# Hybrid decoder layer: inverse softmax sums turned through memory instead of by TensorE, grouped values and scores, new order tables

## Chip, cores and metric

One core of one Trainium2 chip. The metric is the device time of one execution in microseconds (us). The kernel before takes 304.36 us, the median of 3 runs (304.03 to 304.5).

## What is computed

One pre-norm decoder layer over 256 tokens of width 1024, 16 heads of 64. Eight heads (group 0) do causal attention, since one block of 256 keys is all there is; eight heads (group 1) do a mixture of three dilated windows, which here is one softmax with a mask that carries the logarithm of how many windows see a key.

```python
h = rmsnorm(x, attn_norm)
qkv = einsum('bsd,de->bse', h, w_in)            # 1024 x 3072
q, k = rope(q), rope(k)
o_moba = moba_attention(q[:8], k[:8], v[:8])    # group 0
o_dil = dilated_mixture(q[8:], k[8:], v[8:])    # group 1
mixed = concatenate([rmsnorm(o_moba, ...), rmsnorm(o_dil, ...)])
x = x + mixed @ w_out                           # 1024 x 1024
h = rmsnorm(x, ffn_norm)
x = x + (silu(h @ w_gate) * (h @ w_up)) @ w_down   # 1024 x 2816, 2816 x 1024
return rmsnorm(x, final_norm)
```

## The kernel before

**Weights.** All weights stream as blocks of 128 x 512 through a ring of 12 slots (`raw`), four blocks (a quad, 1 MB) per transfer, issued by SyncE (`quad`, L363). Each pair of blocks is split in two rounded parts: ScalarE writes `w_hi` (`split_hi`, L725), VectorE `w_lo`, the rest (`split_lo`, L939). For each block and each half of the tokens TensorE makes three matmuls of 512 columns (`three_pass`, L437 to L439): a block is six of them. Blocks 0 to 47 are the q/k/v projection, 48 to 63 the output projection (group 0 in 48 to 55, group 1 in 56 to 63; of every four blocks all first halves come before all second halves), from 64 on the feed-forward part. A quad is loaded once VectorE has split the last pair that its slots held.

**Attention between the blocks.** The tables `PE_PLAN`, `DVE_PLAN`, `ACT_PLAN` and `PLACE` say behind which block (or slot of the loop that splits pairs) an engine does an item of attention. In the slot of odd number i ScalarE splits pair (i+9)/2, VectorE pair (i+7)/2, after the items of that slot; TensorE needs pair p for block 2p. The items, for group g:

- `rope` (VectorE), `turn` (TensorE transposes q or k, L464; ScalarE and VectorE split the result), `score` u = 0, 1, 2 (TensorE L485 to L490; VectorE adds the mask and takes the maximum, L1032; ScalarE takes the exponential and its sums, L820).
- `squares` (VectorE, L1043): transposes the 32 x 32 squares of one of 12 tiles of probabilities; SyncE then gathers that tile with four transfers of 64 KB (`place_probs`, L403) into one of six landing places.
- `values` (TensorE, L511): values times probabilities, u = 0 for the first half of the tokens, u = 1, 2 for the second. Both halves use bank 7, so each must be taken out before the next is written.
- `rsum`: the inverse of the softmax sums. VectorE inverts (L1048), GpSimd widens them to 128 x 512 (L1234), TensorE transposes them by four transposes (L525), ScalarE copies them to `rsums_turned` (L829). Four times in all (two groups, two halves).
- `norm` (VectorE, L1054): values times `rsums_turned`. `o` (ScalarE L836, L842) and `olo` (VectorE, L1067) split the result; GpSimd adds its squares; `osum` (TensorE, L532) sums them over the features.
- `residual` (VectorE, L1078) adds an output-projection result to `x`; `ffnturn` transposes it for the feed-forward part (TensorE L447, ScalarE L744, VectorE L950).

Every engine works strictly through its own list: an item that waits holds all splits and items behind it.

Of the kernel before, what the change touches and what calls it, by code (L numbers as in the profile page):

```python
# [24 lines left out]
P = 128  # L25
# [40 lines left out]
RSUM_BANK = 7, 6  # L66
# [17 lines left out]
SQ = 32  # L84
# [33 lines left out]
    43: [("values", 0, 1), ("values", 0, 2)],
    45: [("score", 1, 2), ("rsum", 1, 0)],
    50: [("values", 1, 0)],  # L120
    51: [("osum", 0), ("rsum", 1, 1)],
    54: [("values", 1, 1), ("values", 1, 2)],
    58: [("osum", 1)],
    61: [("ffnturn", 0), ("ffnturn", 1)],
# [19 lines left out]
    34: [("turn", 1, 0, 1), ("rsum", 0, 1)],
    37: [("turn", 1, 1, 0)],
    39: [("turn", 1, 1, 1), ("score", 1, 0)],
    40: [("squares", 1, 0), ("squares", 1, 1)],
    41: [("rsum", 1, 0), ("norm", 0, 0), ("score", 1, 1)],
    42: [("squares", 1, 2)],
    43: [("squares", 1, 3), ("norm", 0, 1)],  # L150
    44: [("olo", 0, 0)],
    45: [("score", 1, 2), ("olo", 0, 1)],
    48: [("squares", 1, 4), ("rsum", 1, 1), ("squares", 1, 5)],
    49: [("norm", 1, 0)],
    50: [("osum", 0), ("residual", 0)],
    51: [("olo", 1, 0)],
    53: [("norm", 1, 1), ("olo", 1, 1)],
    54: [("residual", 1)],
    56: [("osum", 1), ("residual", 2)],
    60: [("ffnturn", 0), ("ffnturn", 1)],  # L160
    61: [("residual", 3)],
# [3 lines left out]
    11: [("scale", 0)],  # L165
    12: [("scale", 1)],
    15: [("turn", 0, 0, 0)],
    17: [("turn", 0, 0, 1)],
    21: [("turn", 0, 1, 0)],
    23: [("turn", 0, 1, 1)],  # L170
    24: [("score", 0, 0)],
    27: [("score", 0, 1)],
    28: [("score", 0, 2)],
    30: [("turn", 1, 0, 0)],
    36: [("turn", 1, 0, 1)],
    37: [("rsum", 0, 0)],
    38: [("turn", 1, 1, 0), ("rsum", 0, 1), ("turn", 1, 1, 1)],
    39: [("take", 0)],
    42: [("score", 1, 0)],
    43: [("o", 0, 0), ("score", 1, 1)],  # L180
    44: [("o", 0, 1)],
    46: [("take", 1), ("score", 1, 2)],
    48: [("rsum", 1, 0), ("rsum", 1, 1), ("o", 1, 0)],
    52: [("o", 1, 1)],
    61: [("ffnturn", 0), ("ffnturn", 1)],
    62: [("residual", 2)],
# [13 lines left out]
def build(nc, x, first, weights, gains, final_norm, table, out):  # L200
# [3 lines left out]
    with ctx:  # L204
# [35 lines left out]
        sums = sb("sums", [P, 2, SH, GH])  # L240
        rsums = sb("rsums", [P, 2, SH, GH])
# [116 lines left out]


        @block.sync  # L360
        def _(sp):
# [35 lines left out]
            def place_probs(T):  # L397

                sp.wait_ge(p_turned, T + 1)
                if T >= LANDINGS:  # L400
                    sp.wait_ge(valued, (T - LANDINGS) // 2 + 1)
                for i in range(JS):
                    sp.dma_start(landed[:, T % LANDINGS, i, :],  # L403
                                 p_squares[i * SQ:(i + 1) * SQ, T % SQUARES, :, :]).then_inc(in_p[T % LANDINGS], 16)

            for r in range(2, HR):
                for pos in range(NQ):
                    ring_quad(r, pos)
                    for T in PLACE.get((r, pos), ()):
                        place_probs(T)  # L410
# [23 lines left out]
        def _(pe):  # L434
# [16 lines left out]
            def item(it):  # L451
# [15 lines left out]
                elif kind == "score":  # L467
# [6 lines left out]
                    if done:  # L474
                        pe.wait_ge(max_ready, done)
# [16 lines left out]
                elif kind == "values":  # L492
# [23 lines left out]
                elif kind == "rsum":  # L516
# [3 lines left out]
                    if n:  # L520
                        pe.wait_ge(rsum_taken, n)
# [808 lines left out]
```

## Time and profile before

| | |
|---|---|
| median of 3 runs | 304.36 us |
| the profiled execution, its own time | 304.51 us |
| its span (first to last instruction) | 302.7 us |
| TensorE busy | 294.1 us, 97% |
| VectorE, ScalarE, GpSimd busy | 67%, 55%, 6% |
| granted TensorE clock, mean | 0.994 |
| bytes moved by DMA | 61.65 MB, 204 GB/s |

The span is cut out of the execution's own time; 1.8 us lie around it. Matmuls overlap each other, so that the starts of two matmuls tell more of the time of one than its duration does.

### The profile page before, as it was taken

How to read it: one execution, taken by the hardware profiler on the slowest of the kernel's cores; microseconds unless marked ns; L12 is line 12 of the kernel's file. 1: busy time of each engine (PE TensorE's matmuls, PEld its weight loads, DVE VectorE, ACT ScalarE, POOL GpSimd, SP SyncE). 2: the span in 40 equal slices, each digit the busy share in tenths (PEclk: the TensorE clock that was granted, in tenths of full speed). 3: DMA queues.
4: the chain of work that ended last, by engine and by line, in shares of the span. 5: the costliest groups of instructions: out<-in, count | busy, mean ns of one | idle time of the engine just before them, and what ended most of it. 6: DMA issues, size and time to landing. Idle time of an engine off the chain costs nothing.

```text
span 302.7 us, 4335 instructions
## 1 busy us (share of the span) xinstructions
PE 294.1 (97%) x1448; PEld 240.0 (79%) x1448; DVE 203.7 (67%) x332; ACT 166.9 (55%) x283; POOL 19.3 (6%) x29
## 2 busy tenths in 40 slices
PE   8999999999999899999999999999999999999992
PEld 4688877887788688888888888888888888888882
DVE  3889999977898589729755555637465655455454
ACT  4877775829686549816554445354363545444224
POOL 0011000030333120200000000000000000000010
PEclk9999999999999999999999999999999999999997
DMA  7998445851695535765876566575656564651003
GB/s 255 422 423 302 178 178 141 266 140 79 172 372 177 187 135 150 277 236 210 269 266 207 226 186 264 173 241 174 207 176 249 174 267 159 238 200 28 0 0 139
DMA packets 21757, 61.65 MB, mean 204 GB/s; under 512 B 2545, under 2 KB 13809, under 8 KB 15601
## 3 DMA queue, kind: packets, MB, share of 16 engines
q1 hardware_dynamic: 21312, 60.70, 57.5%
q10 hardware_dynamic: 432, 0.80, 0.7%
q8 instruction: 7, 0.11, 0.1%
q14 instruction: 6, 0.04, 0.0%
HBM read 54.67 MB, written 1.05 MB: 184 GB/s over the span
## 4 chain that ended last, share of the span: by engine, by line
PE 82%; ACT 5%; DMA 5%; issue 3%; DVE 2%; SPq 2%; POOL 0%; POOLq 0%; ACTq 0%; DVEq 0%
PE bank L437 27%; PE bank L439 26%; PE bank L438 26%; DMA raw<-in_weights 2%; DMA room<-in_first 2%; ACT w_hi L725 1%; SPq L403 1%; DMA room<-room 1%; ACT probs L820 1%; PE bank L464 1%; ACT vals L793 1%; PE bank L447 1%; DVE xs L1152 0%; ACT o_hi L836 0%; DVE w_lo L939 0%
## 5 line engine op out<-in xcount | busy, mean ns | idle before, releaser
L725 ACT ACTIVATE w_hi<-raw 128x1024 fp32r<-128x1024 f32 x94 | 98.0, 1056 | 81.2 <-PE bank L439 72.2
L939 DVE TENSOR_TENSOR w_lo<-raw,w_hi 128x1024 fp32r<-128x1024 f32 x94 | 112.3, 1217 | 17.1 <-ACT w_hi L725 15.7
L437 PE MATMUL bank<-w_hi,x_hi 128*128 128x512 f32 x270 | 106.8, 396 | 0.6 <-DVE w_lo L967 0.6
L439 PE MATMUL bank<-w_hi,x_lo 128*128 128x512 f32 x270 | 105.2, 390 | 0.0
L438 PE MATMUL bank<-w_lo,x_hi 128*128 128x512 f32 x270 | 105.2, 390 | 0.0
L437 PEld LDWEIGHTS bank<-w_hi,x_hi 128*128 128x128 f32 x270 | 50.7, 188 | 12.3 <-DVE w_lo L967 1.4
L439 PEld LDWEIGHTS bank<-w_hi,x_lo 128*128 128x128 f32 x270 | 50.7, 188 | 10.6
L438 PEld LDWEIGHTS bank<-w_lo,x_hi 128*128 128x128 f32 x270 | 50.7, 188 | 10.1
L437 PE MATMUL bank<-w_hi,h_hi 128*128 128x512 f32 (+1 forms) x82 | 31.6, 385 | 0.0
L439 PE MATMUL bank<-w_hi,h_lo 128*128 128x512 f32 (+1 forms) x82 | 31.5, 384 | 0.0
L438 PE MATMUL bank<-w_lo,h_hi 128*128 128x512 f32 (+1 forms) x82 | 31.5, 384 | 0.0
L1095 DVE SCALAR_TENSOR_TENSOR rope_a<-bank,rstd,rope_b 128x256 f32<-128x256 f32 x22 | 9.8, 480 | 30.3 <-ACT rope_b L862 30.3
L1113 DVE TENSOR_TENSOR h_lo<-room,h_hi 128x512 fp32r<-128x512 f32 x10 | 6.9, 692 | 23.2 <-ACT h_hi L867 23.2
L437 PEld LDWEIGHTS bank<-w_hi,h_hi 128*128 128x128 f32 x82 | 15.4, 188 | 3.1
L438 PEld LDWEIGHTS bank<-w_lo,h_hi 128*128 128x128 f32 x82 | 15.4, 188 | 3.1
L439 PEld LDWEIGHTS bank<-w_hi,h_lo 128*128 128x128 f32 x82 | 15.4, 188 | 3.0
L820 ACT ACTIVATE probs<-probs,neg_max 128x128 f32<-128x128 f32 (+1 forms) x32 | 14.1, 447 | 4.6 <-DVE neg_max L1032 4.6
L437 PE MATMUL bank<-w_hi,o_hi 128*128 128x512 f32 (+1 forms) x42 | 16.5, 392 | 0.0
L439 PE MATMUL bank<-w_hi,o_lo 128*128 128x512 f32 (+1 forms) x42 | 16.0, 380 | 0.0
L438 PE MATMUL bank<-w_lo,o_hi 128*128 128x512 f32 (+1 forms) x42 | 15.9, 379 | 0.0
L862 ACT ACTIVATE rope_b<-bank,rstd 128x256 f32<-128x256 f32 x22 | 9.6, 464 | 4.1 <-PE bank L439 4.1
L1210 POOL TENSOR_SCALAR msq<-ssq 128x2 f32<-128x2 f32 (+1 forms) x2 | 0.4, 192 | 175.3 <-ACT junk L754 175.3
(101 smaller groups left out, 245.6 us busy)
## 6 DMA issues: line engine op xcount, KB each, us to landing
raw<-in_weights SPq DMA_DIRECT2D x47, 1024.0 KB, 4.8
room<-room SPq DMA_DIRECT2D x88, 64.0 KB, 2.1
room<-in_first SPq DMA_DIRECT2D x3, 384.0 KB, 5.1
room<-in_first SPq DMA_DIRECT2D x1, 1024.0 KB, 7.5
xs<-in_x SPq DMA_DIRECT2D x2, 512.0 KB, 9.3
out<-rot SPq DMA_DIRECT2D x3, 256.0 KB, 2.0
room<-in_first SPq DMA_DIRECT2D x1, 640.0 KB, 8.6
vals<-in_final_norm ACTq DMA_DIRECT2D x1, 512.0 KB, 7.2
```

The source lines that it names most:

```text
L403: sp.dma_start(landed[:, T % LANDINGS, i, :], p_squares[i * SQ:(i + 1) * SQ, T % SQUARES, :, :]).then_inc(in_p[T % LANDINGS], 16)
L437: pe.matmul(dst, a_hi, w1, start=first, stop=False)
L438: pe.matmul(dst, a_hi, w2, start=False, stop=False)
L439: return pe.matmul(dst, a_lo, w1, start=False, stop=last)
L447: ins = pe.transpose(dst[:, a * SEQ + s * P:a * SEQ + (s + 1) * P], xs[:, s, kt * P:(kt + 1) * P], ident)
L464: ins = pe.transpose(bank[TURN_BANK[qk_i][s]][:, p * P:(p + 1) * P], rot[:, qk_i, s, p * P:(p + 1) * P], ident_ja if qk_i else ident)
L725: act.activation(w_hi[:, slot:slot + 2, :], raw[:, slot:slot + 2, :], ACT.Copy).then_inc(hi_ready, 1)
L820: ins = act.activation(piece, piece, ACT.Exp, bias=neg_max[:, g, half, head:head + 1], scale=-1.0, accum_out=sums[:, g, half, head:head + 1])
L862: act.activation(silu[:, s, :], bank[4 + s][:, 0:FC], ACT.Silu, scale=rstd[:, 6 + s:7 + s]).then_inc(silu_done, 1)
L939: dve.tensor_tensor(w_lo[:, slot:slot + 2, :], raw[:, slot:slot + 2, :], w_hi[:, slot:slot + 2, :].bitcast(f32), ALU.subtract).then_inc(lo ...
L1095: dve.scalar_tensor_tensor(hid[:, s, :], bank[4 + s][:, FC:2 * FC], rstd[:, 6 + s:7 + s], silu[:, s, :], ALU.mult, ALU.mult).then_inc(hid_ ...
L1113: dve.tensor_tensor(hidden[1], placed, hidden[0].bitcast(f32), ALU.subtract).then_inc(ht_lo, 1)
```

## The change

1. **Inverse sums.** GpSimd's widening, TensorE's four times four transposes and ScalarE's four copies are gone. VectorE inverts, then transposes the 32 x 32 squares of all 32 sums (a 128 x 32 piece, `rsum_squares`). SyncE writes it to a tensor in HBM (`sums_out`, one transfer, pieces of 128 bytes) and reads it back, each row broadcast to 64 partitions (`sums_back`, two transfers of 128 KB, pieces of 512 bytes). `norm` waits for that.
2. **Banks.** The values of the first half go to bank 7, those of the second to bank 6; the late scores (u = 2) go to banks 6 and 7 instead of 4 and 5. So all three `values` of a group stand behind one block, and two `score` stand together.
3. **ScalarE issues** the gathers of the tiles 9 and 11; SyncE keeps the other ten.
4. **All four tables** are laid out anew.

```diff
-RSUM_BANK = 7, 6
+VALUE_BANK = 7, 6
+SCORE_BANKS = (4, 5), (4, 5), (6, 7)
...
 PE_PLAN = {
-    41: [("values", 0, 0), ("score", 1, 1)],
-    43: [("values", 0, 1), ("values", 0, 2)],
+    41: [("values", 0, 0), ("values", 0, 1), ("values", 0, 2)],
+    42: [("score", 1, 1), ("score", 1, 2)],
...
+    53: [("osum", 0), ("values", 1, 0), ("values", 1, 1), ("values", 1, 2)],
...
-    61: [("ffnturn", 0), ("ffnturn", 1)],
+    62: [("ffnturn", 0), ("ffnturn", 1)],
...
 DVE_PLAN = {
+    43: [("olo", 0, 0), ("olo", 0, 1)],
...
+    50: [("norm", 1, 0), ("residual", 0), ("norm", 1, 1)],
...
 ACT_PLAN = {
+    44: [("place", 9)],
+    45: [("take", 1)],
+    47: [("place", 11)],
...
+PLACE = {
...
+    (4, 2): [("back", 2), ("out", 3)],
+    (5, 0): [("place", 10)],
+    (5, 1): [("back", 3)],
 }
...
+        turned_sums = nc.dram_tensor("turned_sums", (2 * SH, SQ, P), f32, kind="Internal")
...
+            def sums_out(n):
+
+                sp.wait_ge(rsum_ready, n + 1)
+                sp.dma_start(turned_sums[n, :, :].rearrange("c (i a) -> i c a", a=SQ),
+                             rsum_squares[:, n, :]).then_inc(out_sums[n], 16)
+
+            def sums_back(n):
+
+                sp.wait_ge(out_sums[n], 16)
+                if n < SH:
+                    sp.wait_ge(turned, 6)
+                else:
+                    sp.wait_ge(o_ready, n - 1)
+                for r in range(2):
+                    sp.dma_start(rsums_turned[64 * r:64 * r + 64, n % 2, :].rearrange("d (p q) -> d p q", q=P),
+                                 turned_sums[n, n * GH + r:(n + 1) * GH:2, :].partition_broadcast(64)).then_inc(in_sums[n], 16)
...
                     if u == 0:
                         pe.wait_ge(v_taken, 2 * g + 2)
-                        pe.wait_ge(rsum_taken, 2)
-                    if u in (0, 1) and g + u:
-                        pe.wait_ge(o_ready, g * 2 + half)
+                    if g and u == 0:
+                        pe.wait_ge(max_ready, 2 * SC_TILES)
+                    elif u == 1 and not g:
+                        pe.wait_ge(qk_lo, 8)
...
-                                dst = bank[7][64 * r:64 * r + 64, head // 2 * P:(head // 2 + 1) * P]
+                                dst = bank[VALUE_BANK[half]][64 * r:64 * r + 64, head // 2 * P:(head // 2 + 1) * P]
...
-                elif kind == "rsum":
-                    _, g, s = it
-                    n = g * 2 + s
-                    pe.wait_ge(rsum_wide, n + 1)
...
-                    for p in range(HPAIRS):
-                        ins = pe.transpose(bank[RSUM_BANK[g]][:, p * P:(p + 1) * P], rsums_wide[s][:, p * P:(p + 1) * P], ident)
-                    ins.then_inc(rsum_turned, 1)
...
-                    act.activation(rsums_turned[:, s, :], bank[RSUM_BANK[g]][:], ACT.Copy).then_inc(rsum_taken, 1)
...
+                elif kind == "place":
+                    T = it[1]
+                    act.wait_ge(p_turned, T + 1)
+                    act.wait_ge(valued, (T - LANDINGS) // 2 + 1)
+                    for i in range(JS):
+                        act.dma_start(*place(T, i)).then_inc(in_p[T % LANDINGS], 16)
...
-                    dve.reciprocal(rsums[:, g, half, :], sums[:, g, half, :]).then_inc(rsum_ready, 1)
+                    n = g * 2 + half
+                    dve.wait_ge(inverted, n + 1)
+                    dve.reciprocal(rsums[:, g, half, :], sums[:, g, half, :]).then_inc(inverted, 1)
+                    dve.wait_ge(inverted, n + 2)
+                    dve.transpose(rsum_squares[:, n, :], rsums[:].rearrange("p g s h -> p (g s h)")).then_inc(rsum_ready, 1)
...
-                    dve.wait_ge(rsum_taken, n + 1)
+                    dve.wait_ge(in_sums[n], 32)
                     dve.wait_ge(valued, g * 3 + (3 if half else 1))
-                    dve.tensor_tensor(o_sb[:, g, half, :], bank[7][:], rsums_turned[:, half, :],
+                    dve.tensor_tensor(o_sb[:, g, half, :], bank[VALUE_BANK[half]][:], rsums_turned[:, half, :],
```

TensorE in the output projection, blocks 50 to 55, before: a `values` item is rows L511, the sum of squares L532, the transposes of the widened sums L525.

```order
L511 MATMUL bank<-room,vals 64x128 x8
L437 MATMUL bank<-w_hi,o_hi 128x512
...
L532 MATMUL bank<-ones,rot 128x1 x2
L525 MATMUL bank<-tab,rope_b 128x128 x4
L437 MATMUL bank<-w_hi,o_hi 128x512
...
L511 MATMUL bank<-room,vals 64x128 x16
```

And of the change, behind block 53 (L473 to L475 are the matmuls of `three_pass`, L560 the sum of squares, L550 the values):

```order
L473 MATMUL bank<-w_hi,o_hi 128x512
L474 MATMUL bank<-w_lo,o_hi 128x512
L475 MATMUL bank<-w_hi,o_lo 128x512
L560 MATMUL bank<-ones,rot 128x1 x2
L550 MATMUL bank<-room,vals 64x128 x24
L473 MATMUL bank<-w_hi,o_hi 128x512
```

The transposes L525 are gone, and the three `values` of group 1 have become one row of 24.

SyncE's queue before, quads 15 to 17 counted from 0 (L363 a quad, L403 a gather of a tile, four transfers):

```order
L363 DMA raw<-in_weights 128x2048 [waits lo_ready]
L403 DMA room<-room 128x1x128 [waits valued,p_turned]
L403 DMA room<-room 128x1x128 x3
L403 DMA room<-room 128x1x128 [waits valued,p_turned]
L403 DMA room<-room 128x1x128 x3
L363 DMA raw<-in_weights 128x2048 [waits lo_ready]
L403 DMA room<-room 128x1x128 [waits valued,p_turned]
L403 DMA room<-room 128x1x128 x3
L363 DMA raw<-in_weights 128x2048 [waits lo_ready] x6
```

And of the change (L378 a quad, L436 a gather, L415 `sums_out`, L426 `sums_back`):

```order
L426 DMA rot<-turned_sums 64x4x128 [waits o_ready,out_sums2]
L426 DMA rot<-turned_sums 64x4x128
L415 DMA turned_sums<-rsum_squares 4x32x32 [waits rsum_ready]
L378 DMA raw<-in_weights 128x2048 [waits lo_ready]
L436 DMA room<-room 128x1x128 [waits valued,p_turned]
L436 DMA room<-room 128x1x128 x3
L378 DMA raw<-in_weights 128x2048 [waits lo_ready]
L426 DMA rot<-turned_sums 64x4x128 [waits o_ready,out_sums3]
L426 DMA rot<-turned_sums 64x4x128
L378 DMA raw<-in_weights 128x2048 [waits lo_ready] x6
```

The last two returns of the sums now stand directly behind a quad; two gathers have left this queue.

ScalarE of the change at the end of the q/k/v projection, slots 43 to 47 (L753 splits a pair, L869 a gather, L821 takes the values of group 1 out of their bank):

```order
L753 ACTIVATE w_hi<-raw 128x1024 [waits blk_done,raw_full1]
L869 DMA room<-room 128x1x128 [waits valued,p_turned]
L869 DMA room<-room 128x1x128 x3
L821 ACTIVATE vals<-bank,rstd 128x512 [waits rstd_ready,blk_done]
L821 ACTIVATE vals<-bank,rstd 128x512
L753 ACTIVATE w_hi<-raw 128x1024 [waits blk_done,raw_full1]
L869 DMA room<-room 128x1x128 [waits valued,p_turned]
L869 DMA room<-room 128x1x128 x3
L753 ACTIVATE w_hi<-raw 128x1024 [waits blk_done,raw_full2]
```

Before, no gather stood on ScalarE, and the pairs followed each other with only arithmetic between them.

## Rows read from the trace of the kernel before

**Rows 1.** The page's head and busy time of each engine (share of the span).
```profile
span 302.7 us, 4335 instructions
PE 294.1 (97%) x1448; PEld 240.0 (79%) x1448; DVE 203.7 (67%) x332; ACT 166.9 (55%) x283; POOL 19.3 (6%) x29
```

**Rows 2.** Waits of TensorE over the span: us in total, times, longest.
```profile
PE bank L597 <- DVE warm L934: 1.2, 1, 1.2
PE bank L511 <- DMA room<-room: 0.9, 1, 0.9
PE bank L437 <- DVE w_lo L967: 0.6, 1, 0.6
```

**Rows 3.** Busy time by stretch, 60 to 110 us (clock, DMA share, GB/s last).
```profile
60.00:110.00 50.00, 48.96 (x326) 39.57 (x325) 39.39 (x88) 32.85 (x77) 13.14 (x14) 1.00 0.53 172
```

**Rows 4.** Timeline of TensorE, 64 to 68 us: start, us, instruction.
```profile
64.20 0.39 PE L439 MATMUL bank<-w_hi,x_lo 128*128 128x512 f32 x1
...
65.56 0.39 PE L439 MATMUL bank<-w_hi,x_lo 128*128 128x512 f32 x1
65.79 0.60 PE L464 MATMUL bank<-tab,rot 128*128 128x128 f32 x4
66.23 0.60 PE L525 MATMUL bank<-tab,rope_a 128*128 128x128 f32 x4
66.67 0.60 PE L464 MATMUL bank<-tab,rot 128*128 128x128 f32 x4
...
67.33 0.40 PE L438 MATMUL bank<-w_lo,x_hi 128*128 128x512 f32 x1
```

**Rows 5.** Timeline of TensorE around its values items, 77 to 101 us.
```profile
77.66 0.39 PE L439 MATMUL bank<-w_hi,x_lo 128*128 128x512 f32 x1
78.17 1.97 PE L511 MATMUL bank<-room,vals 128*64 128x128 f32 x32
...
80.41 0.39 PE L438 MATMUL bank<-w_lo,x_hi 128*128 128x512 f32 x1
...
91.02 0.39 PE L439 MATMUL bank<-w_hi,o_lo 128*128 128x512 f32 x1
91.34 1.09 PE L511 MATMUL bank<-room,vals 128*64 128x128 f32 x16
...
92.70 0.40 PE L438 MATMUL bank<-w_lo,o_hi 128*128 128x512 f32 x1
...
100.92 1.09 PE L511 MATMUL bank<-room,vals 128*64 128x128 f32 x16 [0.92 <-DMA room<-room]
```

**Rows 6.** VectorE's groups by shape: count, busy us, mean ns, idle before.
```profile
L939 DVE TENSOR_TENSOR w_lo<-raw,w_hi 128x1024 fp32r<-128x1024 f32 x94 | 112.3, 1217 | 17.1 <-ACT w_hi L725 15.7
L1043 DVE STREAM_TRANSPOSE room<-probs 128x512 f32<-128x512 f32 x12 | 8.3, 699 | 1.7 <-ACT probs L820 1.7
L1067 DVE SCALAR_TENSOR_TENSOR o_lo<-room,gain,o_hi 128x128 fp32r<-128x128 f32 x16 | 6.3, 455 | 1.4 <-ACT o_hi L836 1.4
L1032 DVE CUSTOM_DVE_ANT_0 probs<-bank,tab 128x256 f32<-128x256 f32 x16 | 5.8, 417 | 0.0
```

**Rows 7.** Gathers L403 issued at 75 to 78, then 79 to 82 us: time to landing.
```profile
DMA to landing us min/median/max: 2.0/2.1/2.2
...
DMA to landing us min/median/max: 4.1/4.3/4.9
```

**Rows 8.** SyncE's issues, 93 to 98 us: start, us, transfer, count.
```profile
93.96 0.59 SPq L363 DMA_DIRECT2D raw<-in_weights  x1
95.04 2.49 SPq L403 DMA_DIRECT2D room<-room  x4
```

**Rows 9.** Timeline of the turn to the feed-forward part, 112 to 116 us.
```profile
112.10 1.04 PE L447 MATMUL bank<-tab,xs 128*128 128x128 f32 x8
...
112.74 1.57 ACT L744 ACTIVATE x_hi<-bank,gain 128x256 fp32r<-128x256 f32 x4 [3.90 <-PE bank L447]
...
113.91 1.66 DVE L950 SCALAR_TENSOR_TENSOR x_lo<-bank,gain,x_hi 128x256 fp32r<-128x256 f32 x4
```

More of the change, by code:

```diff
@@ L118 @@
-    43: [("values", 0, 1), ("values", 0, 2)],
[L119 to L122, printed above, removed]
+    24: [("score", 0, 1), ("score", 0, 2)],
+    32: [("turn", 1, 0, 0), ("turn", 1, 0, 1)],
+    33: [("turn", 1, 1, 0)],
+    36: [("score", 1, 0)],
+    38: [("turn", 1, 1, 1)],
+    41: [("values", 0, 0), ("values", 0, 1), ("values", 0, 2)],
+    42: [("score", 1, 1), ("score", 1, 2)],
+    53: [("osum", 0), ("values", 1, 0), ("values", 1, 1), ("values", 1, 2)],
@@ new lines @@
+    22: [("squares", 0, 1), ("rope", 1, 0, 0)],
+    23: [("score", 0, 1), ("score", 0, 2)],
+    24: [("squares", 0, 2), ("rsum", 0, 0)],
+    26: [("rope", 1, 0, 1)],
+    28: [("squares", 0, 3), ("rope", 1, 1, 0)],
+    29: [("rsum", 0, 1), ("turn", 1, 0, 0)],
+    31: [("squares", 0, 4), ("turn", 1, 0, 1)],
+    32: [("rope", 1, 1, 1)],
+    33: [("score", 1, 0), ("squares", 0, 5)],
+    34: [("turn", 1, 1, 0), ("squares", 1, 0)],
+    36: [("squares", 1, 1), ("turn", 1, 1, 1)],
+    37: [("norm", 0, 0), ("rsum", 1, 0)],
@@ new lines @@
+    39: [("norm", 0, 1)],
+    41: [("score", 1, 1), ("score", 1, 2)],
+    42: [("squares", 1, 2), ("squares", 1, 3)],
+    43: [("olo", 0, 0), ("olo", 0, 1)],
+    44: [("rsum", 1, 1), ("squares", 1, 4)],
+    47: [("squares", 1, 5)],
+    49: [("osum", 0)],
+    50: [("norm", 1, 0), ("residual", 0), ("norm", 1, 1)],
+    51: [("olo", 1, 0)],
+    52: [("olo", 1, 1)],
+    57: [("osum", 1), ("residual", 1)],
+    59: [("residual", 2)],
+    60: [("ffnturn", 0)],
+    61: [("ffnturn", 1), ("residual", 3)],
+}
@@ L144 @@
[L144 to L161, printed above, removed]
-}
-ACT_PLAN = {
[L165 to L186, printed above, removed]
+    22: [("score", 0, 1)],
@@ new lines @@
+    26: [("score", 0, 2)],
+    31: [("turn", 1, 0, 0)],
+    35: [("turn", 1, 0, 1), ("turn", 1, 1, 0), ("score", 1, 0)],
+    37: [("take", 0), ("turn", 1, 1, 1)],
+    38: [("o", 0, 0)],
+    41: [("score", 1, 1)],
+    42: [("o", 0, 1), ("score", 1, 2)],
+    44: [("place", 9)],
+    45: [("take", 1)],
+    47: [("place", 11)],
+    48: [("o", 1, 0)],
+    51: [("o", 1, 1)],
+    60: [("ffnturn", 0)],
+    61: [("ffnturn", 1), ("residual", 2)],
+}
+PLACE = {
+    (2, 2): [("place", 0)],
+    (3, 0): [("place", 1)],
+    (3, 1): [("place", 2)],
+    (3, 2): [("out", 0), ("out", 1), ("place", 3), ("place", 4), ("back", 0)],
+    (4, 0): [("place", 5), ("back", 1), ("place", 6)],
+    (4, 1): [("place", 7), ("out", 2), ("place", 8)],
+    (4, 2): [("back", 2), ("out", 3)],
+    (5, 0): [("place", 10)],
+    (5, 1): [("back", 3)],
@@ L357, in build, with place @@
         block = ctx.enter_context(nc.Block())
+        def place(T, i):
+            return landed[:, T % LANDINGS, i, :], p_squares[i * SQ:(i + 1) * SQ, T % SQUARES, :, :]
         @block.sync
```

108 lines of the change are left out of this document (43 added, 65 removed).

## The prediction

> **What bounds the kernel now.** I read the page's first part before anything else: TensorE is busy 294.1 of 302.7 us, VectorE 67%, ScalarE 55%, GpSimd 6% [rows 1]. Then the waits of TensorE: three of any size, together 2.7 us, and only one lies inside the work that the change touches, 0.9 us for a gathered tile of probabilities [rows 2]. In the stretch from 60 to 110 us TensorE is busy 48.96 of 50.00 us at a granted clock of 1.00 [rows 3], so at the full of its two levels, 2.4 GHz. So the time is the sum of TensorE's own list. What leaves that list is gained in full, what only leaves another engine is gained not at all, and what counts against the change is each new place where TensorE has to wait. The starts in the timeline give the unit: six matmuls, one block, take 65.56 - 64.20 = 1.36 us, 0.227 us each [rows 4].
>
> **What leaves TensorE: the transposes of the widened sums.** Between the matmuls that start at 65.56 and 67.33 stand three items of four transposes (turn, sums, turn). Two starts of matmuls would take 0.45 us; the items add 67.33 - 65.56 - 0.45 = 1.32 us, 0.44 us each [rows 4]. Four items of sums go: **-1.76 us**. GpSimd's widening and ScalarE's copies stood beside busy TensorE, and I count them at nothing.
>
> **Fewer places.** A lone `values` item adds 92.70 - 91.02 - 0.45 = 1.23 us, two together 80.41 - 77.66 - 0.45 = 2.30 us [rows 5]. By that, standing alone costs 0.16 us extra; by the busy times (1.97 for two, 1.09 for one, so 0.88 for the second) it costs 0.35. The middle, 0.25, is what I take for every place where the blocks are interrupted. The `values`, the u = 1 and u = 2 `score` items and the first `osum` stood in eight places and stand in four; the turns stand in six before and after. Four times 0.25: **-1.0 us** (0.6 to 1.4).
>
> **The wait that is there.** The last `values` of group 1 waited 0.92 us for tile 11 [rows 5], whose gather was issued behind a quad: the quad at 93.96, the gather at 95.04, TensorE goes on at 100.92, so 6.96 us after the quad was issued [rows 8, 5]. Its release is earlier now, since ScalarE issues it. This wait goes, **-0.92 us**; what is late next at that place is below.
>
> **New waits.** With nothing waiting, the parts so far put the output projection's first block at 85.3 us (87.2 before), block 50 at 86.7, block 54 at 97.2, block 56 at 99.9 and the feed-forward part at 112.2 (115.7 before). The lists of the other engines are held against that. Most items have one to four us to spare; three places are tight.
>
> *Pair 25, for block 50.* It follows, on VectorE, the late scores, two transposes and both `olo` of group 0. Counted from the moment that TensorE has finished score (1, 1): eight pieces of score at about 0.35 (the 0.42 of [rows 6] overlap a little), 2.8 us; two splits at 1.15, two transposes at 0.63 (starts of operations in a row lie some 0.08 closer than their durations), eight `olo` at 0.26 to 0.40 (their mean is 0.455, and they overlap too) [rows 6]: 2.8 + 2.3 + 1.3 + 2.1 to 3.2 = 8.5 to 9.6 us. TensorE gets there after score (1, 2), 0.9, five blocks, 6.8, and two half blocks, 1.36: 9.1 us. The wait is 0 to 0.5 us; I take **+0.2**.
>
> *The last values and the last `norm`, behind block 53.* ScalarE's list: pair 26, gather 9 (four issues, which on SyncE take 2.49 us [rows 8]), the values of group 1, pair 27, gather 11, pair 28. That ends gather 11's issues at about 93.1 us, and TensorE wants the tile at 95.9. Landing takes 2.1 us when nothing is ahead and up to 4.9 us behind a quad [rows 7]: 95.2 to 98.0, so 0 to 2.1 us of wait. SyncE's last return of the sums stands behind quad 16, which waits for VectorE's pair 27 at 91.8; with the 6.5 us that a gather so placed needs from the issue of the quad (its last part lands 4.3 to 4.9 after 2 us of issuing [rows 7]) it lands at 98.3. Behind it come `norm` (0.6) and `olo` (1.1 to 1.9): block 56 gets its left operand at 100.4 instead of 99.9. The two waits overlap, since the first moves block 56 as well. Bounds 0 and 2.1; I take **+0.8**, nearer the row without a quad, for the gather has its own queue.
>
> *The feed-forward part.* Before, the turn started at 112.10 and ScalarE at 112.74; four `x_hi` take 1.57, four `x_lo` 1.66 [rows 9]. The first two `x_lo` can be ready 0.64 + 0.8 + 0.1 + 0.8 = 2.35 us after the start of the turn. It stood two blocks and more ahead of the feed-forward part and now stands one block ahead: 0.8 for the turn and 1.36, 2.16 us. **+0.2** (0.1 to 0.5).
>
> The other additions lie beside free engines: four small transposes on VectorE (under 0.2 us each by the size of [rows 6]), and eight transfers of 128 KB and four of 16 KB more, where the DMA engines are half busy [rows 3]. The first three returns of the sums are issued two us or more before they are needed and I give them nothing; without that cover VectorE would stand in `norm` with the next pair behind it.
>
> **Sum.** -1.76 - 1.0 - 0.92 + 0.2 + 0.8 + 0.2 = -2.5 us. The profiled execution's own time of 304.51 becomes 302.0. It stands 0.15 above the median, 304.36, so the prediction against the median is **301.9 us**.
>
> **Rivals.**
> *No new wait.* The three tight places are each computed to within half a us, and VectorE and ScalarE idle a third of the time between them [rows 1]. Then 304.36 - 3.7 = 300.7 us. Against it: the lists are now closer to each other than anywhere in the trace before. Chance 0.20.
>
> *The gathers on ScalarE land no sooner than behind the quad.* Gathers issued behind a quad landed after 4.1 to 4.9 us instead of 2.1 [rows 7], and quad 16 is on its way when gather 11 is issued. If its queue does not matter, the tile comes at 98.0 and the wait behind block 53 is 2.1, not 0.8 us: 303.2 us. The Trainium skill says the same of queues (DMA: Bandwidth & Descriptors, "Issuing engines are not separate DMA queues"): transfers of all issuing engines run on the same 16 DMA engines and interleave, and a second issuer saves only issue time. No row before has a gather from ScalarE beside a quad, so the trace neither bears it out nor speaks against it. Chance 0.16.
>
> *The returns of the sums are slow: slower than before.* Here one value goes to HBM in pieces of 128 bytes and comes back as 512 pieces of 512 bytes, with two landings in a row, and no row shows either. VectorE stands in the last `norm` until then, with pair 29 and both `olo` behind it, and TensorE waits for those at block 56. It decides from a landing at 97.8 us on, one us for one us. To eat the 3.7 us it must land after 101.5, 9 us after its issue, twice the longest landing of [rows 7]; 306 us if all four are that slow. Chance 0.07.
>
> *VectorE falls behind elsewhere*, by a us or two between blocks 20 and 40, where pairs 18 and 20 have 1 to 2 us to spare: 302.8 to 304.5 us. Chance 0.05.
>
> **How the numbers follow.** The forecast has 0.52 (301.2 to 302.6 us by its bounds). The range 300.6 to 303.5 us takes in the case without waits and the one with late gathers, and leaves out the slow returns and most of the last case, a little over 0.1, and what I have not seen. A measurement of this kernel can tell 0.2%, 0.6 us, from no change. Faster by more than that means under 303.75: all of the forecast, the first two rivals and part of the last, 0.86. Within: 0.07. Slower: 0.07.
>
> **What would show it.** Each step: the rows of the transposes of sums gone from TensorE, 16 fewer; one row of 48 `values` matmuls behind block 41 and one behind 53; TensorE's waits at the first `values` group absent and in their place a wait on a landing inside the second group of 48, a short one at block 50 on `w_lo`, one at block 56 on `o_lo`, one at block 64 on `x_lo`; the last return landing near 98 us and `norm` waiting for it rather than for TensorE. The prediction is wrong if TensorE waits more than 2 us at any one place, if a place with several items costs as much as those items did apart, or if a wait stands before block 48.

## The result, and the profile after

The changed kernel takes 306.85 us (median of 20 runs, 304.38 to 308.85), the kernel before 304.24 us (20 runs, 303.63 to 305.3): a ratio of 1.0076, 95% interval 1.0053 to 1.0099. It is slower by 2.6 us where 2.4 us less were forecast, and outside the range. The profiled execution took 308.41 us, near the slow end of its runs. The 20 runs spread over 4.5 us, and those with a lower mean granted clock are mostly the longer ones (0.985 at 308.41, 0.999 at 304.68).

The head of the page after, with the strip of TensorE's clock:

```profile
span 306.3 us, 4307 instructions
...
PE 294.3 (96%) x1432; PEld 241.0 (79%) x1432; DVE 204.2 (67%) x337; ACT 164.2 (54%) x279; POOL 13.3 (4%) x25
...
PEclk9999999999999599999999999999999999999998
```

Against [rows 1], TensorE has 16 instructions fewer and yet is busy 0.2 us more, in a span 3.6 us longer. In one slice, the 14th of 40, the granted clock is half. TensorE's waits, which answer to [rows 2]:

```profile
PE bank L550 <- DMA room<-room: 4.5, 1, 4.5
PE bank L625 <- DVE warm L961: 1.2, 1, 1.2
PE bank L473 <- DVE w_lo L967: 0.4, 1, 0.4
```

A single wait on a transfer takes 4.5 us where 0.9 stood. Its place, in TensorE's timeline (start, us, instruction; "room<-room" is a gather; it answers to [rows 5]):

```profile
70.91 0.39 PE L475 MATMUL bank<-w_hi,x_lo 128*128 128x512 f32 x1
71.22 2.84 PE L550 MATMUL bank<-room,vals 128*64 128x128 f32 x48
...
74.33 0.40 PE L474 MATMUL bank<-w_lo,x_hi 128*128 128x512 f32 x1
...
86.06 0.50 PE L473 MATMUL bank<-w_hi,o_hi 128*128 128x512 f32 x1 [0.40 <-DVE w_lo L967]
...
93.42 1.97 PE L550 MATMUL bank<-room,vals 128*64 128x128 f32 x32
99.91 1.98 PE L550 MATMUL bank<-room,vals 128*64 128x128 f32 x16 [4.51 <-DMA room<-room]
...
102.83 0.63 PE L475 MATMUL bank<-w_hi,o_lo 128*128 128x512 f32 x1
...
110.59 0.50 PE L560 MATMUL bank<-ones,rot 128*128 128x1 f32 x4
```

Group 0's values stand as one row of 48. Group 1's break off after 32, behind block 53, for tile 11. When it has come, 16 matmuls take 1.98 us instead of the 1.09 of [rows 5], and those of 512 columns 0.63 instead of 0.39. By stretch (the columns of [rows 3]):

```profile
60.00:110.00 50.00, 45.08 (x286) 36.71 (x285) 38.42 (x86) 29.71 (x71) 7.40 (x9) 0.93 0.62 194
102.00:105.00 3.00, 3.00 (x8) 2.33 (x9) 3.00 (x7) 2.28 (x6) 0.41 (x1) 0.50 0.00 0
105.00:108.00 3.00, 3.00 (x13) 2.44 (x12) 3.00 (x6) 3.00 (x4) 0.92 (x2) 0.88 0.72 210
```

For the 5 us behind the wait TensorE is granted 0.50, its lower level of 1.2 GHz; the column of busy time hides the loss, since the slower matmuls count as busy. From the start of the last 16 values to the second `osum` the trace takes 110.59 - 99.91 = 10.68 us. Three traces below, with waits of 0.8 to 1.2 us at this place, take 7.97 to 8.00. So the loss is 4.5 us of waiting and 2.7 us of slow clock.

What tile 11 waited behind. First SyncE's issues, for [rows 8]: L378 the quads of weights (1 MB; these are quads 14, 15, 16 and, at 104.89, 17), L436 gather 10, L415 the write of the sums, L426 their returns.

```profile
83.95 0.58 SPq L378 DMA_DIRECT2D raw<-in_weights  x1
84.63 1.36 SPq L426 DMA_DIRECT2D rot<-turned_sums  x2
86.39 0.58 SPq L415 DMA_DIRECT2D turned_sums<-rsum_squares  x1
87.39 0.33 SPq L378 DMA_DIRECT2D raw<-in_weights  x1
87.84 2.99 SPq L436 DMA_DIRECT2D room<-room  x4
90.88 0.77 SPq L378 DMA_DIRECT2D raw<-in_weights  x1
91.74 1.36 SPq L426 DMA_DIRECT2D rot<-turned_sums  x2
104.89 0.33 SPq L378 DMA_DIRECT2D raw<-in_weights  x1
```

Then gather 11 on ScalarE, its first three parts and its last by themselves (durations in ns, first and last start, and time to landing, for [rows 7]):

```profile
L869 ACTq DMA_DIRECT2D room<-room x3: 550/629/1527, 88.7 to 90.9; - x3
...
DMA to landing us min/median/max: 4.4/5.0/5.2
...
L869 ACTq DMA_DIRECT2D room<-room x1: 647/647/647, 91.5 to 91.5; - x1
...
DMA to landing us min/median/max: 8.3/8.3/8.3
```

The last part is issued at 91.5 and lands 8.3 us later, at 99.8, and TensorE goes on at 99.91. It was not issued late: the prediction had 93.1. It landed late, and it alone: the other three were down by 95.3. Three quads go out 3.5 us apart, at 83.95, 87.39 and 90.88, and land after 5.4, 6.6 and 8.7 us. The last part is the only one issued behind the third, quad 16, and lands 0.2 us after it.

Three quads in a row, 3.3 us apart, stood in the kernel before as well, with gathers issued behind the third (first SyncE's issues, then those gathers):

```profile
78.39 0.59 SPq L363 DMA_DIRECT2D raw<-in_weights  x1
...
81.61 0.63 SPq L363 DMA_DIRECT2D raw<-in_weights  x1
...
84.90 0.59 SPq L363 DMA_DIRECT2D raw<-in_weights  x1
...
L403 SPq DMA_DIRECT2D room<-room x4: 543/604/681, 85.6 to 87.5; - x4
...
DMA to landing us min/median/max: 4.5/5.0/5.6
```

There the third quad took 7.6 us and the parts behind it 4.5 to 5.6, and nothing waited for them; the next quad came 9 us later [rows 8]. New in the change are the returns of the sums and a second gather at the same time, and that TensorE soon needs a part issued behind the third quad. The DMA engines after (last two columns: their busy share and GB/s):

```profile
84.00:88.00 4.00, 3.60 (x16) 2.65 (x15) 3.97 (x10) 3.32 (x6) 0.00 (x0) 1.00 0.87 272
88.00:92.00 4.00, 4.00 (x19) 3.33 (x18) 1.79 (x3) 0.00 (x0) 0.00 (x0) 1.00 1.05 346
92.00:96.00 4.00, 3.39 (x42) 2.94 (x40) 2.39 (x4) 1.60 (x3) 1.62 (x1) 1.00 1.05 380
```

and the kernel before, in the same 12 us:

```profile
84.00:88.00 4.00, 4.00 (x20) 3.39 (x21) 4.00 (x17) 3.65 (x8) 0.82 (x1) 1.00 1.07 392
88.00:92.00 4.00, 4.00 (x28) 3.14 (x28) 4.00 (x6) 4.00 (x12) 2.07 (x3) 1.00 0.74 270
92.00:96.00 4.00, 4.00 (x28) 3.36 (x25) 2.55 (x5) 1.70 (x6) 0.88 (x2) 1.00 0.45 100
```

Before, they were full for 4 us and then half empty. After, they are full from 88 to 96 us, with gather 11 on its way from 88.7 to 99.8.

The theory to be tested: the bunched quads fill the DMA engines, so gather 11 lands some 4 us late whoever issues it, and TensorE's idling then drops its clock. The rivals: ScalarE's queue is slow; the last return of the sums is what loads the engines (or delays the release); the clock falls by something else than idling, such as the bunched transfers.

### The profile page after: what moved, and what is told of

Read it like the earlier page. It is cut to its first block, busy times and chain, and to the rows that moved or that the text cites. A ratio compares the mean times of both kernels' runs of the same rounds, so it can differ in the third digit from the quotient of the medians.

```text
span 306.3 us, 4307 instructions
## 1 busy us (share of the span) xinstructions
PE 294.3 (96%) x1432; PEld 241.0 (79%) x1432; DVE 204.2 (67%) x337; ACT 164.2 (54%) x279; POOL 13.3 (4%) x25
## 4 chain that ended last, share of the span: by engine, by line
PE 87%; DVE 5%; DMA 3%; issue 2%; ACTq 1%; ACT 0%; POOL 0%; POOLq 0%; DVEq 0%
PE bank L473 27%; PE bank L475 27%; PE bank L474 27%; DMA room<-room 3%; DVE w_lo L967 2%; PE bank L625 1%; PE bank L500 1%; PE bank L550 1%; DVE o_lo L1099 1%; ACTq L869 1%; DVE probs L1060 1%; PE bank L523 1%; DVE room L1071 1%; PE bank L483 1%; DVE xs L1184 0%
## 5 line engine op out<-in xcount | busy, mean ns | idle before, releaser
L753 ACT ACTIVATE w_hi<-raw 128x1024 fp32r<-128x1024 f32 x94 | 97.5, 1054 | 81.8 <-PE bank L475 72.8
L473 PE MATMUL bank<-w_hi,x_hi 128*128 128x512 f32 x270 | 106.5, 395 | 0.0
L475 PE MATMUL bank<-w_hi,x_lo 128*128 128x512 f32 x270 | 105.2, 390 | 0.0
L473 PEld LDWEIGHTS bank<-w_hi,x_hi 128*128 128x128 f32 x270 | 50.7, 188 | 11.6 <-DVE x_lo L978 0.7
L475 PEld LDWEIGHTS bank<-w_hi,x_lo 128*128 128x128 f32 x270 | 50.7, 188 | 10.8
L473 PE MATMUL bank<-w_hi,h_hi 128*128 128x512 f32 (+1 forms) x82 | 31.6, 385 | 0.0
L475 PE MATMUL bank<-w_hi,h_lo 128*128 128x512 f32 (+1 forms) x82 | 31.5, 384 | 0.0
L475 PEld LDWEIGHTS bank<-w_hi,h_lo 128*128 128x128 f32 x82 | 15.4, 188 | 3.1
L473 PEld LDWEIGHTS bank<-w_hi,h_hi 128*128 128x128 f32 x82 | 15.4, 188 | 3.0
L473 PE MATMUL bank<-w_hi,o_hi 128*128 128x512 f32 (+1 forms) x42 | 17.1, 408 | 0.4 <-DVE w_lo L967 0.4
L474 PE MATMUL bank<-w_lo,o_hi 128*128 128x512 f32 (+1 forms) x42 | 16.7, 397 | 0.0
L475 PE MATMUL bank<-w_hi,o_lo 128*128 128x512 f32 (+1 forms) x42 | 16.6, 396 | 0.0
L550 PE MATMUL bank<-room,vals 128*64 128x128 f32 x96 | 6.8, 300 | 4.5 <-DMA room<-room 4.5
```

The costliest lines, as they stand in the source:

```text
L473: pe.matmul(dst, a_hi, w1, start=first, stop=False)
L474: pe.matmul(dst, a_hi, w2, start=False, stop=False)
L475: return pe.matmul(dst, a_lo, w1, start=False, stop=last)
L550: ins = pe.matmul(dst.rearrange("p (i b) -> p i b", b=SQ), vals[:, g, b, head * HEAD_DIM:(head + 1) * HEAD_DIM], landed[:, T % LANDINGS, : ...
L753: act.activation(w_hi[:, slot:slot + 2, :], raw[:, slot:slot + 2, :], ACT.Copy).then_inc(hi_ready, 1)
```

## The experiments

Each is judged by its ratio to runs of the kernel before in the same job (medians there 304.2, 304.29 and 304.49 us).

**Gather 11 back on SyncE, behind quad 16** (`e1_gather11_sync`); entry 47 is one of ScalarE's plan.
```diff
-    47: [("place", 11)],
-    (5, 1): [("back", 3)],
+    (5, 1): [("place", 11), ("back", 3)],
```


> The changed kernel with the gather of tile 11 back on SyncE, behind quad 16 and ahead of the last return of the sums. Three theories of the 4.5 us wait of TensorE inside the second group of values. A (load): quads 14, 15 and 16 are issued 3.5 us apart, and with two returns and three gathers they keep the 16 DMA engines full, so whatever is issued last lands last; then the gather on SyncE, issued at about 92 to 94 us, lands at 98.5 to 100, the wait stays 3 to 5 us and the time at 305.5 to 308. B (the return): re-reading four rows of 512 bytes for 64 partitions holds everything up; the gather is now ahead of it, so it lands by 97.5, wait under 2 us, time 303 to 304. C (ScalarE's queue is served poorly beside SyncE's): wait 1.5 to 2.5 us, time about 303.5, and the last return lands later than in the changed kernel.

307.3 us, ratio 1.0100 (1.0026 to 1.0175): as slow as the change. Its wait, in TensorE's timeline:

```profile
99.16 1.98 PE L549 MATMUL bank<-room,vals 128*64 128x128 f32 x16 [3.03 <-DMA room<-room]
```

The issues of quad 16 and of the gather, in SyncE's timeline, and the gather's landing:

```profile
91.61 0.59 SPq L377 DMA_DIRECT2D raw<-in_weights  x1
92.30 2.49 SPq L435 DMA_DIRECT2D room<-room  x4
...
L435 SPq DMA_DIRECT2D room<-room x4: 548/603/604, 92.3 to 94.2; - x4
...
DMA to landing us min/median/max: 4.1/4.7/4.9
```

The gather comes 0.7 us behind the quad, the wait is 3.03 us, and the 16 matmuls behind it also take 1.98. But it comes about in another way than in the change: all four parts are issued behind the quad, the last at 94.2 instead of 91.5, and each lands after 4.1 to 4.9 us, within the bounds of [rows 7]. This tile is late because it is issued late; no part takes 8 us. So this run by itself does not clear ScalarE's queue (`f1_two_quads_held` does), and moving the gather to ScalarE gains nothing that these runs can tell. What the two traces share is that the last part lands just after the quad ahead of it, whichever engine issued it: 99.8 and 99.6 in the change, 99.0 and 97.9 here. The Trainium skill has the rule (DMA: Bandwidth & Descriptors, "Issuing engines are not separate DMA queues") that transfers of all issuing engines run on the same 16 DMA engines and interleave, and the two traces agree with it.

**No last return** (`e2_no_last_return`). It leaves out the last return of the sums, so the values of group 1's second half are scaled by what stood in `rot`; SyncE waits later for the transfer out instead.
```diff
-    (5, 1): [("back", 3)],
+            sp.wait_ge(out_sums[3], 16)
             ring_quad(HR, 0)
-                    dve.wait_ge(in_sums[n], 32)
+                    if n < 3:
+                        dve.wait_ge(in_sums[n], 32)
```


> The changed kernel without the last return of the sums (its two transfers of 128 KB are left out, and the last norm takes what lies there, so the second half of group 1 is not normalised right). A: 256 KB of some 1.5 MB are gone, worth about 0.9 us of full DMA engines, so the wait falls from 4.5 to 3 to 4 us. B: the wait falls under 1 us and the time to about 302. C: no change of the wait.

305.03 us over 10 runs, 301.79 to 307.99. The ratio on record, 0.9989 (0.9949 to 1.0028), leaves out the three runs above 306.3 us; by the median of all ten it is 305.03 / 304.2 = 1.003. The profile, at 302.66 us, has a wait of 1.01 for tile 11, where the load theory had expected 3 to 4. In it the last part of gather 11 went out at 91.3 us, 0.3 ahead of quad 16 (91.58), and landed after 5.6 us, so that the short wait can come from that order as well as from the missing return. Without the return the time still reaches 308, in runs at a clock of 0.985 to 0.99: the return is not the whole cause. That it is a part of it is likely, since the fastest runs, 301.79 and 301.93, lie 2.4 us and more under the fastest of the change, 304.38, but one trace doesn't show it.

**Quad 16 held until tile 11 has landed** (`e3_quad16_held`), the return ahead of it.
```diff
-    (5, 0): [("place", 10)],
-    (5, 1): [("back", 3)],
+    (5, 0): [("place", 10), ("back", 3)],
+                    if (r, pos) == (5, 1):
+                        sp.wait_ge(in_p[11 % LANDINGS], 2 * 16 * JS)
                     ring_quad(r, pos)
```


> The changed kernel with quad 16 held on SyncE until tile 11 has landed, and the last return of the sums moved ahead of it. A: gather 11 has only quad 15 and the return beside it, lands by 95.5 us, TensorE's wait at the values is under 0.7 us, its clock does not fall, and the time is 301.3 to 302.5. B: the return is still there just ahead of the gather, so a wait of 3 us or more stays. C: wait of 1.5 us or more stays, since the gather is still on ScalarE's queue behind quad 15.

302.7 us, ratio 0.9947 (0.9930 to 0.9963), runs within 1.1 us of each other. The last values in TensorE's timeline:

```profile
97.88 1.09 PE L551 MATMUL bank<-room,vals 128*64 128x128 f32 x16 [1.20 <-DMA room<-room]
```

The wait is 1.20 us, more than the 0.7 expected, and the 16 matmuls take 1.09 again. With quad 15 still ahead (89.23), gather 11's parts land after 4.9 to 5.7 us.

**The return ahead of quad 16, no hold** (`e4_return_first`).
```diff
-    (5, 0): [("place", 10)],
-    (5, 1): [("back", 3)],
+    (5, 0): [("place", 10), ("back", 3)],
```


> The changed kernel with the last return of the sums moved ahead of quad 16, nothing held. A: the quad leaves 1.5 us or more later, the gather's last parts are issued before or with it: wait 1 to 3 us, time 303 to 305.5. B: the return is now right beside the gather: wait of 4 us or more, 306 or more. C: as the changed kernel, 4 us.

303.18 us over 10 runs (302.26 to 306.11), ratio 0.9974 (0.9950 to 0.9998). Its profile has a wait of 0.82 us: the gather's last part is issued at 91.0 and quad 16 at 92.85. The order alone puts quad 16 behind the return and takes most of the loss away, not reliably: the landing is left to chance where `e3_quad16_held` fixes it.

**Both quads held** (`f1_two_quads_held`): quads 15 and 16 wait for tile 11, gather 10 and the return stand ahead of them.
```diff
-    (4, 2): [("back", 2), ("out", 3)],
-    (5, 0): [("place", 10)],
-    (5, 1): [("back", 3)],
+    (4, 2): [("back", 2), ("out", 3), ("place", 10), ("back", 3)],
+                    if (r, pos) == (5, 0):
+                        sp.wait_ge(in_p[11 % LANDINGS], 2 * 16 * JS)
                     ring_quad(r, pos)
```


> The changed kernel with the gather of tile 10 and the last return of the sums moved ahead of quad 15, and quad 15 (so 16 too) held on SyncE until tile 11 has landed. Load theory (quads issued close together fill the 16 DMA engines): gather 11 now has only quad 14 ahead of it, lands by 95 us, TensorE's wait at the values falls from the 1.2 us of the run with quad 16 held to under 0.5 us, and the time to 301.2 to 302.4. Rival (the gathers on ScalarE's queue are slow in themselves, 5 us or more for their last parts): the wait stays at 1 us or more and the time at 302.7 or above. A third outcome, that quad 15 comes too late for pair 30: a new wait of TensorE on w_lo at block 60.

301.72 us (301.47 to 302.24), ratio 0.9911 (0.9887 to 0.9935). TensorE's timeline:

```profile
93.53 2.84 PE L550 MATMUL bank<-room,vals 128*64 128x128 f32 x48
...
99.50 0.47 PE L473 MATMUL bank<-w_hi,o_hi 128*128 128x512 f32 x1 [0.18 <-issue]
```

Gather 11, its issues and its landing:

```profile
L869 ACTq DMA_DIRECT2D room<-room x4: 584/634/759, 88.8 to 90.9; - x4
...
DMA to landing us min/median/max: 2.4/2.6/2.7
```

The same gather from the same queue at the same time lands after 2.4 to 2.7 us, all 48 values stand in one row, and no wait over 0.5 us is left in TensorE's list but that at the very start. Gather 10 (issued at 88.19) and the last return (91.24) still stand beside it; only the quads 15 and 16 have gone, to 93.3 us. This settles the first half of the theory: the landing was late because of the quads, and neither ScalarE's queue nor the return alone makes it late.

**Gather 11 on SyncE ahead of quad 16, nothing held** (`f2_gather11_sync_ahead`).
```diff
-    47: [("place", 11)],
-    (5, 0): [("place", 10)],
-    (5, 1): [("back", 3)],
+    (5, 0): [("place", 10), ("place", 11), ("back", 3)],
```


> The changed kernel with the gather of tile 11 on SyncE instead of ScalarE, and with both it and the last return of the sums ahead of quad 16, with nothing held. Load theory: the quad leaves at 94 us or later, behind the gather, so the wait at the values is 0.5 to 2 us and the time 302 to 303.5, as with the quad held; it does not matter which engine issues the gather. Rival (ScalarE must issue it): 3 us or more of wait, 305 or more.

302.36 us over 8 runs (302.17 to 306.23), ratio 0.9941 (0.9922 to 0.9961). The profile fell on the slowest run, with a wait of 2.44 us and a clock of 0.988. That wait is one of late issue: SyncE issues gather 10 and gather 11 in a row, the last part leaves at 95.0 us and lands 3.9 later, with quad 16 only behind it (97.04). By the median it does not matter which engine issues the gather; that gather and return stand ahead of the quad does.

**A wait of TensorE forced by other means** (`f3_forced_wait`): `e3_quad16_held`, with the last values made to wait for a later weight load.
```diff
+                    elif g and u == 2:
+                        pe.wait_ge(raw_full[1], 16 * 6)
```


> The kernel with quad 16 held, and TensorE made to wait for the landing of quad 16 before the last values of group 1: the same transfers, a wait of 5 to 7 us instead of 1.2. If the granted clock falls because TensorE idles, it falls here too, with the transfers spread: the stretch from the last values to the second sum of squares takes 10 to 11 us instead of 8.0, and the time is that of the kernel with the quad held plus the longer wait plus 2 to 3 us, 309 to 312. If the fall belonged to the bunched transfers, the stretch stays at 8.0 us and the time is 307 to 308.5.

309.98 us, ratio 1.0183 (1.0160 to 1.0206). The wait, in TensorE's timeline:

```profile
101.63 1.97 PE L553 MATMUL bank<-room,vals 128*64 128x128 f32 x16 [5.02 <-DMA raw<-in_weights]
```

The stretches behind it (the clock is the third column from the end):

```profile
101.00:103.00 2.00, 1.37 (x14) 1.40 (x16) 0.00 (x0) 0.00 (x0) 0.00 (x0) 0.66 0.00 0
103.00:105.00 2.00, 2.00 (x10) 1.38 (x7) 1.29 (x4) 0.56 (x2) 0.00 (x0) 0.50 0.00 0
105.00:109.00 4.00, 4.00 (x19) 3.34 (x18) 4.00 (x8) 4.00 (x8) 1.34 (x2) 0.99 0.28 84
```

The transfers are spread as in `e3_quad16_held`, TensorE idles 5.02 us instead of 1.20, and the clock falls as in the change. From the last values to the second `osum` it takes 9.51 us instead of 7.97. The two profiles differ by 308.86 - 303.49 = 5.4 us: 3.8 of wait and 1.5 of clock. The medians differ by more, 7.3 us; the profiled run was the fastest of its four, and the other three have a mean clock of 0.983 to 0.984 instead of 0.988. The expected 10 to 11 us for the stretch were not reached in the trace, the expected time was. It is the idling that costs the clock, not the bunched transfers.

**The sums again through TensorE** (`f4_sums_by_tensor`), on top of `f1_two_quads_held`: GpSimd widens, TensorE transposes, ScalarE copies, no transfers of the sums.
```diff
-    38: [("turn", 1, 1, 1)],
+    38: [("turn", 1, 1, 1), ("rsum", 0, 0)],
+    39: [("rsum", 0, 1)],
+    45: [("rsum", 1, 0)],
+    52: [("rsum", 1, 1)],
-    (4, 2): [("back", 2), ("out", 3), ("place", 10), ("back", 3)],
+    (4, 2): [("place", 10)],
...
```


> The kernel with two quads held, but the sums turned as before the change: GpSimd widens, TensorE transposes (four items of four), ScalarE copies; no write and no returns; the banks, the joined values and scores and the tables otherwise as changed. By the count of TensorE's work: 1.4 to 1.8 us slower than the kernel with two quads held, 303.0 to 304.0. If what the change gains lies only in the joined items, no slower than that kernel; if the returns cost TensorE something still, faster.

303.29 us, ratio 0.9958 (0.9940 to 0.9976), 1.57 us more than `f1_two_quads_held`. This prices the term of the sums, forecast at 1.76.

**The two `olo` apart** (`g1_olo_apart`), on top of `f1_two_quads_held`.
```diff
-    43: [("olo", 0, 0), ("olo", 0, 1)],
-    44: [("rsum", 1, 1), ("squares", 1, 4)],
+    43: [("olo", 0, 0)],
+    44: [("olo", 0, 1), ("rsum", 1, 1), ("squares", 1, 4)],
```


> The kernel with two quads held, and VectorE's second olo of group 0 moved one slot back, behind the split of pair 25. If pair 25 is late only because both olo stand ahead of it, TensorE's 0.4 us wait on w_lo at block 50 goes and nothing takes its place: 301.2 to 301.5. If the second olo is then late for the second half of block 48: a wait there of as much, no gain.

301.57 us (301.01 to 303.14), ratio 0.9925 (0.9898 to 0.9952). The wait at block 50 is gone from its trace. The time can't be told from `f1_two_quads_held`; of the versions run these two are the fastest.

**The kernel before, with gather 11 ahead of the quad** (`g2_before_gather_ahead`).
```diff
-PLACE = {(3, 0): (0,), (3, 1): (1,), (3, 2): (2, 3, 4, 5), (4, 0): (6,), (4, 1): (7,), (4, 2): (8,), (5, 0): (9, 10), (5, 1): (11,)}
+PLACE = {(3, 0): (0,), (3, 1): (1,), (3, 2): (2, 3, 4, 5), (4, 0): (6,), (4, 1): (7,), (4, 2): (8,), (5, 0): (9, 10, 11)}
```


> The kernel before, with one entry moved: the gather of tile 11 ahead of quad 16 instead of behind it. The 0.9 us wait at the last values should go: 303.3 to 303.7. It tells how much of what the repaired change gains could have been had without it.

303.4 us, ratio 0.9970 (0.9960 to 0.9981). The wait of [rows 5] is gone, and 0.3% (0.9 us by the ratio) with it. `f1_two_quads_held` gains 0.9% (2.7 us), so a third of that was to be had without any of the rest.

**One place more for the scores, one for the values** (`g3_two_seams`), on top of `f1_two_quads_held`.
```diff
-    24: [("score", 0, 1), ("score", 0, 2)],
+    23: [("score", 0, 1)],
+    24: [("score", 0, 2)],
-    53: [("osum", 0), ("values", 1, 0), ("values", 1, 1), ("values", 1, 2)],
+    52: [("values", 1, 0)],
+    53: [("osum", 0), ("values", 1, 1), ("values", 1, 2)],
```


> The kernel with two quads held, with score (0, 1) moved one block forward, to 23, and values (1, 0) to 52, so that two of the joined places are split again. By the estimate of 0.25 us for each place at which the blocks are interrupted (bounds 0.16 and 0.35): 0.3 to 0.7 us slower than the kernel with two quads held, about 302.2. If an item costs the same wherever it stands, no difference.

303.8 us, ratio 0.9980 (0.9970 to 0.9991): 2.1 us more for two places, but no clean price. TensorE's waits in its profile:

```profile
PE bank L475 <- DVE w_lo L997: 1.2, 1, 1.2
PE bank L627 <- DVE warm L963: 1.2, 1, 1.2
PE bank L475 <- issue: 1.1, 1, 1.1
PE bank L475 <- DVE w_lo L969: 0.4, 1, 0.4
```

The first is a wait at the start of 1.2 us instead of 0.5, which has nothing to do with the places. The third, at 102.02 us behind the moved values, is 0.9 us longer than in `f1_two_quads_held`; whether the move made it stays open. The two scores, by the starts around them, add 2.24 us apart and 1.83 together, 0.4 for that place.

## Why the prediction was wrong

**The step that failed is "the last values and the last `norm`", +0.8 us with bounds 0 and 2.1.** It measured 4.5 us of wait and 2.7 of clock. The work ahead of it was right or a little early: the issues of gather 11 are over at 88.72 + 3.44 = 92.2 (93.1 forecast), and TensorE wants the tile at 93.42 + 1.97 = 95.4 (95.9). What failed is the landing. I bounded it by the rows with no quad ahead and with one [rows 7], 2.1 and 4.9 us, and took a value near the first "for the gather has its own queue". The row with one quad came from the start of a series of three, at 78.39, 81.61 and 84.90 us; behind the third, a part already took 5.6 us and the quad itself 7.6, and the prediction uses neither. In the new order, with returns of the sums and two gathers beside the three quads, the DMA engines were full for 8 us. The last part of gather 11 went out 0.6 us behind quad 16, and both landed late, after 8.3 and 8.7 us. The prediction itself said that quad 16 waits for pair 27 at 91.8 us, and had gather 11's issues end at 93.1; that puts the last part behind the quad, and so its landing at that of a third quad in a row. I treated the load on the DMA engines as "half busy [rows 3]", a mean over 50 us, for a question of 8. `f1_two_quads_held` shows it by taking the quads away: 2.4 to 2.7 us.

**The clock was in no term.** A wait was priced one us for one us. `f3_forced_wait` shows that one of 5 us costs 1.5 us on top, and the change's own 2.7. My condition, "more than 2 us at any one place", did name what came true.

**The rival of late gathers** had the place right and its size wrong: it gave a wait of 2.1 us, still from [rows 7], and so 303.2 us. The slower rival, the returns, named the wrong transfer: TensorE waited for tile 11, and the last return, landing 6.3 to 7.8 us after its issue at 91.7 to 92.4, by 100.2 at the latest, was there before the last values ended (101.89). It was late as well, though: 98.3 was forecast, and by the prediction's own count it costs time from 97.8 on. With tile 11 in time it would have been next. With it ahead of quad 16 (`e4_return_first`), or left out (`e2_no_last_return`), the wait is about 1 us in the profiles; how much of that is its load, and how much the order of the gather's last part and quad 16, these two don't separate.

**The chances:** the forecast and the first two rivals add up to 0.88, not to the 0.86 given for "faster".

**The sums, -1.76 us:** right. Sixteen transposes are gone, and bringing them back costs 1.57 us (`f4_sums_by_tensor`).

**Fewer places, -1.0 us (0.6 to 1.4):** too small, about -1.7. If all gaps between starts of 512-column matmuls beyond 0.227 us are added up, the places with values, scores and `osum` take 11.6 us before (the wait of 0.92 left out) and 9.9 in `f1_two_quads_held`, 0.4 for each of the four places. The low price of 0.16 came from a tainted row: in [rows 5] the 32 matmuls start 78.17 - 77.66 = 0.51 us after the one ahead, the lone 16 91.34 - 91.02 = 0.32, so a short stall of 0.19, too small for the list of waits, stood in the pair. The other price, 0.35 by busy times, was the better one. Group 0's three values now add 74.33 - 70.91 - 0.45 = 2.97 us, against 1.23 + 2.30.

**The wait that is there, -0.92 us:** right, and more easily had (`g2_before_gather_ahead`).

**Block 50, +0.2 us:** the place and the releaser right, the wait 0.40. With the restart, two starts take 86.39 - 85.27 = 1.12 instead of 0.45 us, so it costs 0.67: a wait interrupts the stream as a place does. **The feed-forward part, +0.2 us:** the first start of the feed-forward part, at 118.98, is 0.3 us late by the same count. In `f1_two_quads_held` the wait at block 56 is there as well, 0.35.

**The sum for both.** From 304.51: -1.76 - 1.7 - 0.92, - 0.48 because the first turn comes earlier (24.81, against 28.01 less two blocks of 1.36), + 0.67 + 4.5 + 2.7 + 0.3, and + 0.3 because the time around the span is 2.11 instead of 1.81: 308.1, of 308.41. That `f1_two_quads_held` with 301.72 comes out near the change's forecast of 301.9 is partly luck: the places gain 0.7 us more, the 0.8 behind block 53 is down to 0.35 at block 56, and against that block 50 costs 0.5 more and 0.3 more lies around the span. **Absolute times** up to block 48 in my text were about one block late (85.3; it starts at 84.13): 0.48 us of it is the earlier first turn, most of the rest the places' larger gain.

## What to carry to other kernels

Before pulling work together, write down when each large load will be issued in the new order (here the third quad went out at 90.88 us, in the middle of the gather that TensorE needed), and bound a small transfer's landing by the loads that will be in flight ahead of it, not by a row from a quieter stretch. Where a small transfer is needed soon and a large one is not, issue the small one first or hold the large one until it has landed. Price a wait of TensorE with the clock it may cost behind it (here 1.3 to 2.7 us for waits of 2.4 us and more), and count a short interruption of its stream as 0.35 to 0.4 us.

## What the hardware showed that I had not expected

- The same gather, parts of 64 KB from the same queue at nearly the same time, landed after 2.4 to 2.7 us with both quads held (`f1_two_quads_held`), 4.9 to 5.7 with one held (`e3_quad16_held`) and 4.4 to 8.3 with none (the change), where only the part behind quad 16 took more than 5.2. Between 96 and 100 us the engines' mean share was back to 0.45 and the last part still landed at 99.8. That some of the 16 lag behind the others would fit; it wasn't tried and stays open.
- TensorE's granted clock fell to 0.50 in the profiles where TensorE had just idled 2.44 us (16 matmuls in 1.82 us), 3.03, 4.51 and 5.02 us, and not after 0.82, 1.01 and 1.20 us. The stretch to the second `osum` took 1.3 to 2.7 us longer for it. Why the loss differs between them is open.
- The change turned a kernel whose 20 runs spread over 1.7 us into one that spreads over 4.5 us; with both quads held the four runs spread over 0.8.
- ScalarE took 3.44 us to issue the four parts of gather 11 in the change (one alone 1.53), and 2.63 to 2.70 in the profiles of `e2_no_last_return`, `e3_quad16_held`, `e4_return_first` and `f1_two_quads_held`; SyncE took 2.49 for four [rows 8]. This may be where the change's spread comes from: with the 0.8 to 0.9 us less, the last part would have left at about 90.7, ahead of quad 16 (90.88), as it did in `e2_no_last_return`. One trace of the change is too few to show it.
